# Turning the sample requests' cached keys with VectorE through DRAM, ahead of a reordered attention stage

## The reference, cut to what matters

```python
# D_MODEL 2048, SEQ 512, DEC_BATCH 8, DEC_SEQ 4, N_MEM 256, X_HEADS 4, X_HEAD_DIM 512, all float32
# cache_mem_k, cache_mem_v: (1, 8, 256, 4, 512)
qx = (h2 @ w_cq).reshape(bsz, t_len, X_HEADS, X_HEAD_DIM)
scores = jnp.einsum('bthd,bmhd->bhtm', qx, mem_k) * (X_HEAD_DIM ** -0.5)
probs = jax.nn.softmax(scores, axis=-1)
ctx = jnp.einsum('bhtm,bmhd->bthd', probs, mem_v).reshape(bsz, t_len, D_MODEL)
x = x + ctx @ w_co
```

## Time and profile before

| | |
|---|---|
| median of three runs | 1666.66 us (1665.84 to 1668.19) |
| profiled execution, span from first to last instruction | 1663.2 us |
| TensorE (PE) busy | 1643.0 us, 99% |
| VectorE (DVE) busy | 969.9 us, 58% |
| ScalarE (ACT) busy | 673.3 us, 40% |
| mean DMA rate | 138 GB/s |

### The profile page before, as it was taken

How to read it: one execution, slowest core, us unless ns; L and a number is a source line. 1 busy time by engine, 2 the same in 40 slices (tenths; PEclk the granted TensorE clock), 3 DMA queues, 4 the chain that set the end, 5 groups by cost and what they waited for, 6 DMA issues and landing times.

```text
span 1663.2 us, 31696 instructions
## 1 busy us (share of the span) xinstructions
PE 1643.0 (99%) x12906; PEld 1522.8 (92%) x12906; DVE 969.9 (58%) x1676; ACT 673.3 (40%) x1146; POOL 183.7 (11%) x191
## 2 busy tenths in 40 slices
PE   7999999999999999999999999999999999999998
PEld 5887899999999999999999999999999987499998
DVE  5776446665756647565433343333887753499952
ACT  5566345254442543435322222222343333344542
POOL 0121001111121112111100001111000000001120
PEclk9999999999999999999999999999999999999999
DMA  7898734243232432333333334444223399733462
GB/s 266 261 295 254 219 92 119 55 109 99 70 99 53 115 91 77 91 84 96 101 81 83 86 104 139 132 132 138 62 87 97 98 388 396 229 103 105 126 187 108
DMA packets 277534, 229.79 MB, mean 138 GB/s; under 512 B 10825, under 2 KB 244178, under 8 KB 271970
## 3 DMA queue, kind: packets, MB, share of 16 engines
q1 hardware_dynamic: 277184, 228.42, 44.9%
q10 hardware_dynamic: 258, 0.09, 0.0%
HBM read 201.31 MB, written 27.53 MB: 138 GB/s over the span
## 4 chain that ended last, share of the span: by engine, by line
PE 92%; DVE 4%; issue 1%; ACT 1%; DMA 1%; POOL 0%; SPq 0%; DVEq 0%; ACTq 0%; POOLq 0%
PE pj L287 48%; PE pj L486 10%; PE pj L2203 7%; PE dk L2203 5%; PE pj L2946 2%; PE dk L2515 2%; PE pj L2539 1%; PE dk L2439 1%; PE dk L1819 1%; PE pj L2450 1%; PE pj L2548 1%; PE dk L1272 1%; PE dk L1278 1%; PE dk L825 1%; PE dk L2975 1%
## 5 line engine op out<-in xcount | busy, mean ns | idle before, releaser
L287 PE MATMUL pj<-a_hi,w_high 128*128 128x272 f32 x1792 | 394.1, 301 | 0.0
L287 PE MATMUL pj<-a_hi,w_low 128*128 128x272 f32 x1792 | 370.4, 288 | 0.0
L287 PE MATMUL pj<-a_lo,w_high 128*128 128x272 f32 x1792 | 369.7, 288 | 0.0
L287 PEld LDWEIGHTS pj<-a_hi,w_high 128*128 128x128 f32 x1792 | 280.9, 189 | 13.4 <-issue 8.1
L271 DVE TENSOR_TENSOR w_low<-w_raw,w_high 128x2048 fp32r<-128x2048 f32 x76 | 173.9, 2288 | 192.7 <-ACT w_high L261 192.6
L287 PEld LDWEIGHTS pj<-a_lo,w_high 128*128 128x128 f32 x1792 | 281.6, 189 | 0.0
L287 PEld LDWEIGHTS pj<-a_hi,w_low 128*128 128x128 f32 x1792 | 280.1, 189 | 0.1
L261 ACT ACTIVATE w_high<-w_raw 128x2048 fp32r<-128x2048 f32 x76 | 145.4, 1913 | 57.9 <-PE pj L287 45.9
L2087 ACT ACTIVATE q_high<-q_part 128x512 fp32r<-128x512 f32 x140 | 77.5, 620 | 73.3 <-DVE q_part L2141 37.0
L287 PE MATMUL pj<-mix_hi,w_high 128*128 128x272 f32 x512 | 105.9, 288 | 0.0
L287 PE MATMUL pj<-mix_lo,w_high 128*128 128x272 f32 x512 | 105.5, 288 | 0.0
(11 more groups left out here) (482 smaller groups left out, 3029.5 us busy)
## 6 DMA issues: line engine op xcount, KB each, us to landing
w_raw<-in_w_in_dram SPq DMA_DIRECT2D x48, 1024.0 KB, 5.9
w_raw_wide<-in_w_ck_dram SPq DMA_DIRECT2D x16, 1024.0 KB, 8.6
w_raw_wide<-in_w_cv_dram SPq DMA_DIRECT2D x16, 1024.0 KB, 7.9
w_raw<-in_w_out_dram SPq DMA_DIRECT2D x16, 1024.0 KB, 6.0
q_part<-in_w_cq_dram SPq DMA_DIRECT2D x48, 256.0 KB, 3.6
w_raw<-in_w_co_dram SPq DMA_DIRECT2D x8, 1024.0 KB, 8.3
q_part<-in_w_co_dram SPq DMA_DIRECT2D x32, 256.0 KB, 3.8
xr<-xT_scratch SPq DMA_DIRECT2D x16, 272.0 KB, 6.3
```

What stands on the lines that cost most here:

```text
L287: mm = pe.matmul(pj[:, 2 * (q % 2) + b, 0:n], wt[:, k, :], x(k, o, n), start=(k == 0 and m == 0), stop=(k == KT - 1 and m == 2))
```

## The change

Sixteen MiB of cached keys are turned before the attention stage, in 22 units, and go to a DRAM scratch `keysT_d` in the layout that the scores need. Ten units of 1 MiB (half a request) take part in the pool branch, groups 1 to 3; twelve of 0.5 MiB in the output projection. In each unit four DMAs load rows as four blocks of 32 partitions, two VectorE transposes (of 32 x 32 blocks) turn them, and eight DMAs store them. Loading, turning and storing of one unit fall into successive tiles. The buffers take the place of `mix_hi` for k = 0 to 5, so the parts of the mixer split are reordered: k = 0 to 5 are now split in the last pool tile, behind the last store of the ten units. The attention stage loads turned keys, has eight slots in place of six, drops the transposes and their copies, and has a new order on all engines. VectorE's loop over output tiles is written out.

```diff
+        keysT_d = nc.dram_tensor("keysT_scratch", [NB, P, KT, MEM], F32, kind="Internal").ap()
...
+        POOL_UNITS = 10
+        OUT_UNITS = 12
+        take = area(M_DELTA + 2 * 2 * P, M_HIMIX + 6 * TOK)
+        kin = take("kin", [BLOCKS, 2 * P])
+        kout = [take(f"kout{i}", [4, BLOCKS, T32]) for i in range(2)]
...
+        def keys_in(sp, dst, b, first, loaded):
+            for i in range(4):
+                cols = slice(first + i * dst.shape[-1], first + (i + 1) * dst.shape[-1])
+                src = t["cache_mem_k"][0, b].rearrange("(g m) h d -> m g (h d)", m=T32)
+                sp.dma_start(dst[i * T32:(i + 1) * T32], src[:, :, cols]).then_inc(loaded.sem, 16)
...
+        def keys_out(sp, src, b, tile, step, first, n, stored):
+            for i in range(4):
+                dst = keysT_d[b, first * T32:(first + n) * T32, tile + step * i, :].rearrange("(j d) m -> d j m", d=T32)
+                sp.dma_start(dst, src[i * T32:(i + 1) * T32].rearrange("p j g m -> p j (g m)")).then_inc(stored.sem, 16)
...
+        def keys_turn(dve, dst, src):
+            return dve.transpose(dst[:].rearrange("p j g m -> p g j m"), src.rearrange("p g (j d) -> p g j d", d=T32))
...
+        def sp_keys(sp, n):
+            if 0 < n <= POOL_UNITS:
+                sp.wait_ge(k_turned.sem, k_turned.at(2 * n))
+                for f in range(2):
+                    keys_out(sp, kout[f], (n - 1) // 2, 8 * ((n - 1) % 2) + f, 2, 0, 4, k_stored[f])
+            if n < POOL_UNITS:
+                if n == 0:
+                    sp.wait_ge(oa_done, HEADS)
+                keys_in(sp, kin, n // 2, 8 * P * (n % 2), k_in_loaded)
...
+        def dve_keys(dve, n):
+            if 0 < n <= POOL_UNITS:
+                dve.wait_ge(k_in_loaded.sem, k_in_loaded.at(64 * n))
+                for f in range(2):
+                    at_least(dve, k_stored[f], 64 * (n - 1))
+                    keys_turn(dve, kout[f], kin[:, :, f * P:(f + 1) * P]).then_inc(k_turned.sem, 1)
...
@@ sp_pool, at the end of each tile of groups 1 to 3
+                    if not first:
+                        sp_keys(sp, 4 * (g - 1) + q)
@@ act_pool
+                    if g == 3 and q == 3:
+                        mix_take_high(act, 3)
-        MIX_PARTS = ((0, 4), (4, 8), (8, 14), (14, 16))
+        MIX_PARTS = ((6, 8), (8, 12), (12, 14), (0, 6), (14, 16))
...
             if m == 3:
+                for s in k_stored:
+                    act.wait_ge(s.sem, s.at(64 * POOL_UNITS))
+                act.wait_ge(k_turned.sem, k_turned.at(2 * POOL_UNITS))
@@ dve_pool
                     if q == 3:
+                        if g == 3:
+                            mix_take_low(dve, 3)
                         dve_windows(dve, g, 0)
+                    if g > 0:
+                        dve_keys(dve, 4 * (g - 1) + q)
@@ sp_out, at the end of each tile; dve_out, behind split_low
+                    sp_keys_late(sp, 4 * j + q)
+                    dve_keys_late(dve, i)
@@ dve_out
-            body(0)
-            with dve.Fori(1, 4) as j:
+            for j in range(4):
                 body(j)
@@ pe_out
-            pe.wait_ge(mix_low, 2)
+            pe.wait_ge(mix_low, 4)
-                    steps = {2: [pe_ux(NG - 1, 1)], 7: [pe_map(NG - 1), split(3)], 13: [split(4)]}
+                    steps = {2: [pe_ux(NG - 1, 1)], 7: [pe_map(NG - 1)], 13: [split(5)]}
@@ sp_cq, from part_done 77 on
-            for m in range(2):
-                load_half(sp, t["cache_mem_k"], 0, m, KEYS_AT)
-            load_half(sp, t["cache_mem_k"], 1, 0, KEYS_AT)
+            sp_ktb(sp, 0)
+            load_keys(sp, 0, 0, 8)
+            load_keys(sp, 0, 8, KT)
+            load_keys(sp, 1, 0, 12)
             sp.wait_ge(part_done.sem, part_done.at(78))
+            load_keys(sp, 1, 12, KT)
+            sp_ktb(sp, 1)
+            load_keys(sp, 2, 0, 8)
+            load_keys(sp, 3, 0, 8)
@@ sp_attention (new, from the loads of the last requests on)
+            for b, scored in ((2, 5), (3, 6), (4, 7)):
+                sp.wait_ge(sk_done.sem, sk_done.at(scored))
+                load_values(sp, b)
+            sp.wait_ge(sk_done.sem, sk_done.at(NB))
+            sp.dma_start(raw[0][:], source("co", 0, 0)).then_inc(w_loaded[0], 16)
+            sp.wait_ge(sc_done.sem, sc_done.at(XH))
+            load_values(sp, 5)
+            load_values(sp, 6)
+            sp.wait_ge(sv_done.sem, sv_done.at(3))
+            load_values(sp, 7)
@@ pe_attention (new order)
+            pe_prompt_scores(pe, 0)
+            scores(0)
+            scores(1)
+            pe_prompt_scores(pe, 1)
+            turn(0)
+            context(0, every)
+            scores(2)
+            scores(3)
+            turn(1)
+            context(1, every)
+            scores(4)
+            pe_prompt_scores(pe, 2)
+            for b in (5, 6, 7):
+                scores(b)
+            pe_prompt_scores(pe, 3)
...
+            turn(2)
+            for b in (0, 1, 2):
+                values(b)
             context(2, every)
+            turn(3)
+            for b in (3, 4, 5):
+                values(b)
             values(6)
-            turn(3)
             values(7)
             context(3, every[0:2])
```

More of the change, by code:

```diff
@@ L1896, in body @@
                         act_ust(act, NG - 1, 1)
[L1897 removed]
+                        mix_take_high(act, 4)
                     i = 4 * j + q
@@ L2325, in build @@
         vtb = [take(f"vtb{i}", [2, XD]) for i in range(2)]
[L2326 to L2343, removed]
+        SLOTS = {"w": M_W, "raw_a": M_RAW, "raw_b": M_RAW + 2 * D, "high": M_HIGH, "hi_end": M_A + 8 * TOK,
+                 "lo_end": M_A + KT * TOK + 8 * TOK, "q_a": M_B, "q_b": M_B + 2 * D}
@@ new lines, in build @@
+        kept_keys = {name: put(f"keys_{name}", [KT, MEM], F32, at) for name, at in SLOTS.items()}
+        kept_values = {name: put(f"values_{name}", [2, D], F32, at) for name, at in SLOTS.items()}
+        kv_loaded = {name: Reused(sem(f"kv_{name}_loaded"), 0) for name in SLOTS if name[0] != "q"}
+        kv_loaded["q_a"], kv_loaded["q_b"] = Reused(mem1_loaded, 16), Reused(st_stored, 96 * HEADS)
+        KEYS_AT = (("w", 1), ("raw_a", 1), ("hi_end", 1), ("lo_end", 1), ("raw_b", 1), ("high", 1), ("w", 2), ("raw_a", 2))
@@ new lines, in build, with load_keys, load_values @@
+        VALUES_AT = (("hi_end", 2), ("lo_end", 2), ("raw_b", 2), ("high", 2), ("w", 3), ("q_a", 1), ("q_b", 1), ("raw_b", 3))
+        def load_keys(sp, b, first, end):
+            slot, _ = KEYS_AT[b]
+            sp.dma_start(kept_keys[slot][:, first:end, :], keysT_d[b, :, first:end, :]).then_inc(kv_loaded[slot].sem, 16)
+        def load_values(sp, b):
+            slot, _ = VALUES_AT[b]
+            for m in range(2):
+                sp.dma_start(kept_values[slot][:, m, :], t["cache_mem_v"][0, b, m * P:(m + 1) * P, :, :].rearrange(
+                    "p h d -> p (h d)")).then_inc(kv_loaded[slot].sem, 16)
@@ L2408, in sp_attention @@
+            sp_ktb(sp, 3)
             sp.wait_ge(cx_done.sem, cx_done.at(4))
             sp_vtb(sp, 2)
[L2410 to L2413, removed]
+            for b, scored in ((0, 3), (1, 4)):
+                sp.wait_ge(sk_done.sem, sk_done.at(scored))
+                load_values(sp, b)
             sp.wait_ge(cx_done.sem, cx_done.at(8))
@@ L2519, in pe_attention, with scores @@
         def pe_attention(pe):
-            pe_sample_keys(pe)
+            def scores(b):
+                loaded(pe, b, KEYS_AT)
+                pe.wait_ge(qm_ready.sem, qm_ready.at(b + 1))
+                for d in range(DT):
+                    for h in range(XH):
+                        mm = pe.matmul(pj[h * NS:(h + 1) * NS, 0, 0:MEM], qmb[b % 2][:, DT * h + d, :],
+                                       kept_keys[KEYS_AT[b][0]][:, DT * h + d, :],
+                                       start=(b == 0 and d == 0), stop=(b == NB - 1 and d == DT - 1))
+                mm.then_inc(sk_done.sem, 1)
             def turn(h):
@@ L2590, in act_attention @@
             act.wait_ge(part_done.sem, part_done.at(7 * GROUPS))
-            for b in range(NB):
-                take_keys(act, b, 0)
             def exps(h):
@@ L2626, in dve_attention @@
             dve.wait_ge(rest_out.sem, rest_out.at(7 * PAIRS))
-            for b in range(NB):
-                queries(dve, b)
-                take_keys(dve, b, 1)
             def maxima(h):
@@ new lines, in dve_attention @@
+            queries(dve, 0)
+            queries(dve, 1)
+            maxima(0)
+            queries(dve, 2)
+            over_sums(0)
+            queries(dve, 3)
+            maxima(1)
+            take_turned(0)
+            for d in range(DT):
+                if d == 2:
+                    over_sums(1)
+                take_context(0, d)
+            queries(dve, 4)
+            queries(dve, 5)
+            take_turned(1)
+            for d in range(DT):
+                take_context(1, d)
@@ new lines, in dve_attention @@
+            queries(dve, 6)
```

(24 more changed lines are left out.)

245 lines of the change are left out of this document (101 added, 144 removed).

## The result

The changed kernel takes **1670.81 us** (median of 11 runs, 1668.13 to 1673.67), beside 1666.66 us of the kernel before (11 runs, 1665.41 to 1668.19). The ratio is 1.0024 with a 95% interval of 1.0017 to 1.0032: slower by 0.24%. The forecast was 1645.5 us, in a range of 1640 to 1656. It was wrong in size and in sign. All runs in the ratios of this document are fast ones; one run of the kernel before, beside the first experiments, took 2987.48 us at a granted clock of 0.81 and is not in them.

What follows compares the result with a forecast made beforehand. TensorE, with a matmul in flight 1643.0 of 1663.2 us, was taken as the bound. -29.0 + 2.5 + 3.0 + 2.5 = -21.0 us gave a span of 1642.2; with 3.5 us carried over, 1645.5 us, range 1640 to 1656.

Steps and rivals of the forecast that it cites:

- The units in the pool and output stages: Pool and output stages: added unit work costs nothing; a pool unit's cycle of 11.5 us fits a 13.3 us tile.
- Landing of the loads: Pool unit cycle: four loads landed 6.0 us after the first load's issue, like a weight tile.
- SP's commands: SP's queue: twelve DMAs a unit at 0.38 us, 4.6 us, costing nothing as weight loads run three tiles ahead.
- about 5 us of a turn's lateness: Pool units: a turn about 5 us late is absorbed before `split_low` is late.
- Rival C: Ten pool units: cycle outruns the tile, a loss above 15.4 us; at 27 us, 140 us lost; chance 0.04.
- Attention: Attention stage: 256 sample-key transposes removed, -29.0 us; waits of 2.5 and 3.0 us added.
- waits at turns and first values: Attention: TensorE waits 1.2 us at head 0, 0.7 at head 1, 0.6 at the first values; 2.5 us together.
- last values: End of attention: last values product wants data at 1426.4, which lands at 1429.4; wait 3.0 us, bounds 0 to 7.9.
- The end of the transfers: Attention loads: 38.8 MB at 418 GB/s from 1334.0, with additions for the weight tile and landing, ending at 1429.4.
- rival A: Attention becomes bound by its transfers: 1656 at 90% of the rate, some 1661 at 358 GB/s; chance 0.15.
- The last pool tile: Last pool tile: mixer split after the stores delays VectorE's windows and the `ux` refill; cost 2.5 us, up to 5 more.
- The output units: Output stage: half units bring the DMA share to 0.73, below one, at no cost.

Runs made afterwards that it cites:

- number 4: Changed kernel with each pool-unit load reading rows of 8 KiB in place of 1 KiB, same commands and bytes: 1657.62 us (one run).
- Number 6: Changed kernel with each pool unit stored by two DMAs of 4 KiB rows in place of eight, same bytes: 1652.77 us (one run).
- number 8: On number 2, the output projection's first weight tile loaded behind the last values: 1645.86 us (4 runs), ratio 0.9876.
- number 2: Changed kernel with SP issuing the next pool unit's four loads ahead of the eight stores: 1648.39 us (4 runs), ratio 0.9884.
- number 9: On number 2, nine pool units and fourteen half units, mixer splits a tile earlier: 1645.41 us (4 runs), ratio 0.9877.

## Why the prediction was wrong

**The step that failed** is "The units in the pool and output stages": "3.0 + 6.0 + 2.5 = 11.5 us. ... Nothing, with 1.8 us to spare." It measured 15.56. Term by term in the cycle shown above:
- Issue of eight stores: 3.0 forecast, 3.9 measured. The 0.38 of the earlier trace rows was that of a load of another tensor; most of these take 0.43 to 0.46, with 0.04 between two.
- Landing of the loads: 6.0 from the first command, 8.5 measured (905.02 to 913.55). The figure was that of one DMA, the weight tile of the earlier trace rows, and was applied to four. The fourth is issued 1.5 us after the first and lands 7.0 us later.
- Turn: 2.5 forecast, 2.4 measured (1.22 us for 128x1024).
- Left out: what SP has queued ahead of the stores, which holds them back by 1.2 us behind the turn of 882.89 and by 1.4 behind that of 944.35; issues of eight stores that take 4.8 and 4.6 us in the first two units; and landings slower than this one (up to 8.0 us). They bring the mean from 14.8 to 15.56. Why the loads land as late as they do is known in part only: longer rows took 1.1 us off the cycle (number 4), the rest is open.

SP's commands were also costed by themselves: twelve of 0.38 us were called "4.6 us, in a queue whose weight loads run three tiles ahead. Nothing". That cover holds for the weight loads, not for the unit's own commands, which no one issues ahead. Number 6 shows them to be on the cycle.

**What the cover was worth.** The prediction took about 5 us of a turn's lateness as absorbed. Lateness of a chain slower than TensorE outgrows any such cover, since it grows by 2.3 us a tile: 20 us over nine. And it came out first at a place that the prediction did not look at: SP waits for the turn, and behind that wait stood `pw`, issued 2.95 us ahead of its map already in the kernel before. The rule to name what is queued behind a new wait was kept for VectorE and broken for SP. It came out again in the last pool tile: the forecast had the tenth unit's stores landed near 961 us; the unit was turned at 975.78, and ScalarE's split began at 984.29 with them in.

**The clock.** No wait was priced with what follows it. Two maps ran 2.4 and 2.3 us longer, the last values product took 3.22 us in place of 1.92, and about 3 us went in the last tile, where the granted clock was 0.73.

**Rival C** named the mechanism, the ten pool units and the point, 15.4 us, from which a gain turns into a loss. It expected the lateness at `split_low`, and not at `pw`. At 15.56 its formula gives 1645.5 + 10 x 2.26 = 1668, and 1670.8 was measured. That it comes so near is in part luck: it counts ten cycles where there are nine, and nothing for the clock. Its chance of 0.04 came from its price: it was argued with a store that lands in 18.8 us, and dismissed with it. The stores land in 2.4 us and are not on the cycle at all. A sum of steps in series should have been compared with 15.4 with the error of each step, and 2.5 us on the landing alone would have brought it to 14.

**Where it was right.** Attention: -29.0, waits at turns and first values 2.9 (2.5 forecast), last values 4.4 and 1.3 for the clock (3.0 forecast), together -20.4 where -21.2 was measured and -23.5 forecast; the 0.8 us between them is not traced. The end of the transfers was forecast at 1429.4 for an attention that starts at 1342.9, some 97 us after the first load; in the trace it is 97.9 (1358.91 to 1456.76):

```profile
1440.12 16.64 DMA values_raw_b<-in_cache_mem_v_dram
1456.76 0.14 issue
1456.90 3.22 PE pj L2598 x16
```

The rate held, so rival A is out:

```profile
1375.00:1430.00 55.00, 52.88 (x406) 34.34 (x406) 20.18 (x32) 14.69 (x37) 0.00 (x0) 1.00 1.02 418
...
1435.00:1440.00 5.00, 5.00 (x30) 1.77 (x23) 0.03 (x1) 0.60 (x1) 0.00 (x0) 1.00 1.11 335
```

The one dip, to 335 GB/s, is where the weight tile with its short rows comes through, which number 8 moved. The Trainium skill's 358 GB/s, which rival A took for a limit, is by the Trainium skill ("Perfetto Trace Analysis", section Roofline) the share of a core while both cores of a pair use the memory. With one core running, 418 agrees with that.

The last pool tile: 2.5 us forecast, 3.0 of wait in number 2, where the pool stage has no other wait, and number 9 takes it away. The output units: a share of 0.73 forecast, 0.71 measured, no loss. With the cycle out of the way (number 2) the kernel takes 1648.39 us where 1645.5 was forecast, inside the range.

## What to carry to other kernels

Where a load, a turn and a store of one unit share one buffer and one queue, write down the cycle as a sum in series (each command's issue, the landing of the last load from its own issue, the turn) and compare it with the slot; if it is longer, the difference is paid in every unit, wherever it comes out. Issue what the next unit needs (its loads) ahead of what nobody waits for (the stores), and use few commands. When a wait is put into a queue, go through everything behind it, however unrelated, and look for the one with the least slack.

## What the runs showed of the hardware

- The busy share of the DMA engines says little of what they could still carry: 0.92 at 209 GB/s and 0.93 at 240 GB/s in the same stage. The Trainium skill ("Perfetto Trace Analysis", section Identifying the Most-Contended Engine) calls this occupancy misleading for the sixteen engines; the two rows agree.
- An issue by SP is not always short: `spool` took 6.2 us where it had taken 1.6, and the two loads of `values_q_a` at 1430.21 took 8.3. Both came while many transfers were in flight; what holds them was not tried, though by the estimate above the first made 4.6 of the 7.3 us that `pw` was late.
- Rows of 8 KiB in place of 1 KiB took 1.1 us off a cycle in loads (one run); 4 KiB in place of 1 KiB in stores moved nothing beyond a run's spread.
- A wait of 5.1 us of TensorE was followed by a stretch at a granted clock of 0.61 and then 0.71, and cost 2.4 us more than itself.
